# The first weight chunk third in the load stream and split in halves, the first four products filled two input blocks at a time

## What is computed

```python
mod_lat = silu_c @ w_ada[l] + b_ada[l]          # modulation of the 256 tokens
mod_ctx = silu_cc @ w_ada[l] + b_ada[l]         # modulation of the context
sh, sc, gt = jnp.split(mod_lat, 3, axis=-1)
sh_c, sc_c, gt_c = jnp.split(mod_ctx, 3, axis=-1)
xn = _rms_norm(x, g_norm) * (1 + sc[:, None]) + sh[:, None]
cn = _rms_norm(ctx, g_norm) * (1 + sc_c) + sh_c
(au, av, az, bq, bk, bv, bz, cq, ck, cv, co, cz, cg) = _split_proj(xn @ w_in)
(au_c, ..., ck_c, ...)                               = _split_proj(cn @ w_in)
```

## Time and profile before

| | us |
|---|---|
| median of three runs | 1150.38 |
| lowest, highest | 1149.53, 1152.26 |
| the profiled execution | 1150.57 |
| its span in the trace | 1148.6 |
| busy in it: TensorE matmuls | 1093.4 |
| VectorE, ScalarE, GpSimd | 722.2, 590.7, 130.0 |

### The profile page before, as it was taken

One profiled execution on the slowest core, in us unless ns is written; L12 is line 12 of the kernel. 1 busy time (PEld: TensorE's weight loads), 2 busy tenths in 40 slices (PEclk: granted clock), 3 DMA queues, 4 the chain that ended last, 5 costly groups with the idle time before them and its releaser, 6 DMA issues.

```text
span 1148.6 us, 19921 instructions
## 1 busy us (share of the span) xinstructions
PE 1093.4 (95%) x8128; PEld 958.1 (83%) x8128; DVE 722.2 (63%) x1227; ACT 590.7 (51%) x969; POOL 130.0 (11%) x156
## 2 busy tenths in 40 slices
PE   3999999999989999889999999999998999999998
PEld 1787888766767989579888999999997789999997
DVE  4546557376434667766866667666676667766764
ACT  5343666445233567656556555444465536544443
POOL 0000000044020000233223100000012321000000
PEclk9999999999898999989999999999999999999999
DMA  9732112177420433014433345555543233555451
GB/s 371 268 137 79 68 43 74 41 278 270 147 74 1 160 144 116 33 55 157 179 125 114 144 147 221 184 185 182 184 149 119 101 115 143 200 187 200 182 187 54
DMA packets 24426, 167.01 MB, mean 145 GB/s; under 512 B 2832, under 2 KB 3216, under 8 KB 4752
## 3 DMA queue, kind: packets, MB, share of 16 engines
q1 hardware_dynamic: 24336, 165.74, 39.4%
HBM read 164.68 MB, written 1.05 MB: 144 GB/s over the span
## 4 chain that ended last, share of the span: by engine, by line
PE 86%; DVE 5%; ACT 4%; issue 2%; POOL 1%; DMA 1%; SPq 0%; DVEq 0%; ACTq 0%; POOLq 0%
PE bank L426 24%; PE bank L427 23%; PE bank L428 23%; DVE wlo L420 2%; ACT whi L405 2%; PE bank L464 2%; PE bank L1373 2%; PE bank L1506 1%; PE bank L1526 1%; PE bank L1516 1%; PE bank L1400 1%; PE bank L1391 1%; DMA raw<-in_stream 1%; PE bank L479 1%; PE bank L2455 1%
## 5 line engine op out<-in xcount | busy, mean ns | idle before, releaser
L426 PE MATMUL bank<-OPH,whi 128*128 128x256 f32 (+1 forms) x1716 | 526.5, 307 | 5.8 <-DVE wlo L420 3.4
L427 PE MATMUL bank<-OPL,whi 128*128 128x256 f32 (+1 forms) x1716 | 516.7, 301 | 0.0
L428 PE MATMUL bank<-OPH,wlo 128*128 128x256 f32 (+1 forms) x1716 | 516.5, 301 | 0.0
L420 DVE TENSOR_TENSOR wlo<-raw,whi 128x1024 fp32r<-128x1024 f32 x256 | 305.3, 1234 | 109.5 <-ACT whi L405 109.3
L426 PEld LDWEIGHTS bank<-OPH,whi 128*128 128x128 f32 x1716 | 329.3, 192 | 27.8 <-issue 7.6
L427 PEld LDWEIGHTS bank<-OPL,whi 128*128 128x128 f32 x1716 | 329.4, 192 | 12.5 <-issue 1.7
L428 PEld LDWEIGHTS bank<-OPH,wlo 128*128 128x128 f32 x1716 | 329.2, 192 | 11.5
L405 ACT ACTIVATE whi<-raw 128x1024 fp32r<-128x1024 f32 x256 | 255.6, 1049 | 103.8 <-PE bank L428 103.8
L426 PE MATMUL bank<-whi,OPH 128*128 128x256 f32 (+1 forms) x272 | 89.2, 328 | 0.0
L427 PE MATMUL bank<-wlo,OPH 128*128 128x256 f32 (+1 forms) x272 | 87.3, 321 | 0.0
L428 PE MATMUL bank<-whi,OPL 128*128 128x256 f32 (+1 forms) x272 | 87.1, 320 | 0.0
(11 more groups left out here) (284 smaller groups left out, 1167.1 us busy)
## 6 DMA issues: line engine op xcount, KB each, us to landing
raw<-in_stream SPq DMA_DIRECT2D x147, 1024.0 KB, 4.8
PROJ<-in_stream SPq DMA_DIRECT2D x5, 1024.0 KB, 14.9
X<-in_x_in SPq DMA_DIRECT2D x4, 512.0 KB, 6.3
C<-in_con SPq DMA_DIRECT2D x1, 1477.5 KB, 9.1
out<-PROJ SPq DMA_DIRECT2D x4, 256.0 KB, 2.0
WST<-in_w_s SPq DMA_DIRECT2D x2, 256.0 KB, 5.0
PROJ<-in_last_gain SPq DMA_DIRECT2D x1, 512.0 KB, 5.7
BS<-in_b_s SPq DMA_DIRECT2D x1, 256.0 KB, 5.3
```

Of the source, the lines that this page charges most:

```text
L420: nc.vector.tensor_tensor(c.w[1][:, part], c.raw[:, part], c.w[0][:, part].bitcast(F32), ALU.subtract).then_inc(*raises(c.lo[h]))
L426: nc.tensor.matmul(out, w[0], x[0], start=start, stop=False, skip_group_check=skip)
L427: nc.tensor.matmul(out, w[0], x[1], start=False, stop=False, skip_group_check=skip)
L428: return nc.tensor.matmul(out, w[1], x[0], start=False, stop=stop, skip_group_check=skip)
```

## The change

Three things are moved; no instruction is added or taken away.

The stream: weight chunk 0 comes before the two chunks of pair 1 and no longer behind them. Weight chunk 1 stays the sixth.

The split: ScalarE and VectorE split the first half of weight chunk 0 before the operand of pair 0, its second half behind that, the first half of weight chunk 1 before the operand of pair 1 (low part: before `dve_operand(e, 1)`), its second half behind that as before.

TensorE's order: ck0 on blocks (0, 1) goes between the products and the turn of pair 1; ck1, keys and values on (0, 1) follow the turn; then the four products take the next two blocks in turn between the steps of pairs 2 and 3.

```diff
                 pairs[1].multiply(e, 0)
                 pairs[1].multiply(e, 1)
+                first.fill_part(e, ck0, (0, 1))
                 pairs[1].turn(e)
-                for j in (ck0, ck1):
-                    first.fill_part(e, j, (0, 1))
+                first.fill_part(e, ck1, (0, 1))
+                first.fill_part(e, keys, (0, 1))
+                first.fill_part(e, values, (0, 1))
                 pairs[2].multiply(e, 0)
-                for j in (ck0, ck1):
-                    first.fill_part(e, j, (2, 3))
+                first.fill_part(e, ck0, (2, 3))
+                first.fill_part(e, ck1, (2, 3))
                 pairs[2].multiply(e, 1)
-                first.fill_part(e, keys, (0, 1))
+                first.fill_part(e, keys, (2, 3))
                 pairs[2].turn(e)
-                first.fill_part(e, keys, (2, 3))
+                first.fill_part(e, values, (2, 3))
                 pairs[3].multiply(e, 0)
-                first.fill_part(e, values, (0, 1))
+                first.fill_part(e, ck0, (4, 5))
+                first.fill_part(e, ck1, (4, 5))
                 pairs[3].multiply(e, 1)
-                first.fill_part(e, values, (2, 3))
+                first.fill_part(e, keys, (4, 5))
                 pairs[3].turn(e)
-                for j in (ck0, ck1, keys, values):
-                    first.fill_part(e, j, (4, 5))
+                first.fill_part(e, values, (4, 5))
                 for j in (ck0, ck1, keys, values):
                     first.fill_part(e, j, (6, 7))
...
                 pairs[0].copy_rows(e, "act")
+                split_hi(e, 0.5)
                 act_operand(e, 0)
+                split_hi(e, 1)
                 pairs[1].copy_rows(e, "act")
-                split_hi(e, 1)
+                split_hi(e, 1.5)
                 act_operand(e, 1)
                 split_hi(e, 2)
...
                 dve_scale(e, 0)
+                split_lo(e, 0.5)
                 dve_operand(e, 0)
+                split_lo(e, 1)
                 pairs[1].add_bias(e)
                 dve_scale(e, 1)
-                split_lo(e, 1)
+                split_lo(e, 1.5)
                 dve_operand(e, 1)
                 split_lo(e, 2)
...
-        pairs = []
+        pairs, early = [], []
...
-            if i == 1:
-                early = take(2)
+            if i < 2:
+                early += take(1)
...
-            s += [ada[pairs[:4]], w_in[:2], ada[pairs[4:8]], w_in[2:], ada[pairs[8:]],
+            s += [ada[pairs[:2]], w_in[:1], ada[pairs[2:4]], w_in[1:2], ada[pairs[4:8]], w_in[2:], ada[pairs[8:]],
```

## The result

The changed kernel takes 1152.49 us in the median of 20 runs (1148.39 to 1154.22), the kernel before 1149.72 us beside it (1148.50 to 1152.26, 20 runs). The ratio is 1.0019 with a 95% interval of 1.0011 to 1.0026: **2.2 us slower**, within the 0.2% bound but clear of no change. The forecast was 1150.7, 0.3 us over the 1150.38 of its time, so the loss is 1.9 us larger than forecast. The time lies in the stated range, next to the 1152.6 that rival B gave for one spell of low clock.

A forecast was written before the change was run, and what follows sets the result against it. TensorE, busy 95% of the span, was taken as the bound. Keys at 31.25 + 25.72 of work + waits 0.92 + 2.12 = 60.01 against 59.69, +0.3 us: 1150.7 us, range 1148.2 to 1153.8.

The forecast's parts named there:

- rival B: Clock falls in TensorE's new waits (29.3 to 31.25 or 52.4 to 54.5 us): one spell +2.2, 1152.6 us; chance 0.27.
- The mark: Start of the gate product on TensorE, at 59.69 us before the change; forecast 60.01, with nothing behind it edited.
- Part 1: Weight chunk 0 as third load instead of fifth lands at 18.3 us instead of 23.4; pair 1's second chunk at 23.4.
- Part 2: Split in halves on ScalarE and VectorE: first high half fits ScalarE's gap; low operand starts at 24.4 instead of 23.62 us.
- Part 3: TensorE's ck0 ahead of pair 1's turn: turn at 26.9 instead of 24.85, keys wait until 31.25, 1.9 us idle.
- the assumption on the clock: Between 23 and 26.2 us TensorE is busy longer, so the clock holds; a fall there would cost 0.6 us.
- Part 4: TensorE's fills of blocks 4 and 6 come before their low operands: waits of 0.92 and 2.12 us.
- The sum: Start of keys, unchanged work and two operand waits put the gate product at 60.01 against 59.69 us: +0.3 us.
- A: Rival that the forecast's addition up to the gate product holds: 1150.7 us; chance 0.50.
- C: Rival that the operand waits before blocks 4 and 6 do not come: 1147.7 us in full; chance 0.13.
- D: Rival that chunk 0's landing does not follow its new place, holding back ScalarE's first operand: +1.8, 1152.5 at least; chance 0.04.

The follow-up runs named there:

- the last experiment: Eight float32 matmuls that nobody reads put ahead of the first product: on the changed kernel 1152.51 us, ratio 1.0014; on the kernel with early pairs 1147.07 us.

## Why the prediction was right, and where it was not

**The mark and the mechanism.** Right: the difference arises ahead of the gate product, and the 1089 us behind it moved by 0.1. The time came 1.9 us over the forecast, and the range held because it had been drawn wide enough for rival B.

**Part 1, the stream.** Right. In the changed kernel's trace the weight chunk is issued at 5.44 us and takes 12.7 us, landing at 18.1 (18.3 forecast); pair 1's second product starts at 23.19 (23.5 forecast).

**Part 2, the split.** Right. The first high half runs at 19.62 in ScalarE's gap, the low operand starts at 24.11 (24.4).

**Part 3, TensorE's order.** Right in its mechanism, 1.64 us off in size. The turn behind the fill at 27.82, MOD at 29.55 (27.95 forecast), the scaling at 30.03, the low half at 31.62 and keys at 32.89 make the chain that was forecast, link by link; with the clock held it starts keys at 31.03. The sentence that failed is the assumption on the clock: "I take it that the clock holds there", with "0.6 us" if not. The price counted only block k1 and the turn. The fall came earlier, at 22.1 us, in the stretch between pair 1's two products that part 1 itself had opened; so pair 1's second product (0.87 us more) and both blocks of ck0 fell in it as well: the turn started 0.92 us later than forecast, and MOD followed it by 1.73 us instead of 1.05. The reading behind the assumption failed too. The prediction says that the trace of before shows a fall only after long idleness, but there the clock fell at 26.2, 0.3 us after the turn had ended at 25.9; the long wait of 3.37 us had only begun, and what lay behind the fall was an idle stretch of 1.84 us, no longer than the 1.9 and 2.1 us that the new order was forecast to have.

**Part 4, the operands too late.** Right. Both waits came where they were placed, 0.97 and 1.96 us for 0.92 and 2.12, and went in the experiment that moves the turns. From the turn to the fill it was 4.41 us both times, where 4.30 were forecast.

**The sum.** From keys to the mark 28.76 us were forecast and 29.40 measured, though the two waits are 0.11 shorter than forecast. The missing 0.75 us are small terms. The two waits cost more than the profile's idle time: from start to start they add 1.04 and 2.13 us (46.70 less 44.66 and the 1.00 of a product in a running stream; 56.65 less 54.29 and 0.23), 0.24 us over the idle times. Behind both, the two blocks start 0.79 and 0.80 us apart (46.70 and 47.49, 56.65 and 57.45), where three matmuls at 0.228 take 0.68; that makes 0.23 us, which the prediction named, at 0.1 us at most, and left out. The restart at keys and one more change from fills to a product cost about 0.1 us each. The rest, under 0.1 us, is not placed. With 1.64 us from the clock in part 3 that makes 2.28 us, and 60.01 + 2.28 is the measured 62.29.

**The rivals.** B was the one that came, at half of A's chance: a spell of low clock, in a third place. That its +2.2 us is what was measured is partly luck: in the profile the clock cost 1.64 us and not 1.86, and the small terms above, which B did not have, made up the difference and more. It was given 0.27; over the 20 runs only two, at 1148.39 and 1148.65 us, have a mean clock of 0.990, and 15 lie above 1151.9; the median is 1152.5 at a mean clock of 0.987 (eight runs) and 1153.3 at 0.982 (two). Two runs thus lie 2 us under the forecast of A, and no trace tells where their clock held. B's chance should have been the larger. C did not happen; D did not either, and its mechanism is real when the stream is put back.

**The rule on the clock.** The Trainium skill, "TensorE: Matmul & The Clock Gate", section "A second HAM failure mode: psum-queue depth-cycling", has brief idle stretches between groups of matmuls, when they come often enough, make the clock swing between its levels. The traces agree in part. The clock fell in or behind idle stretches of 1.36, 1.87 and 1.96 us, and at none of those places in the profile with all stretches filled. But the changed kernel's own wait of 1.96 us and waits of 1.87 and 1.97 us in the last experiment brought no fall, so the length of the stretch alone does not decide, and what does is open. The prediction took from this rule a time of one or two spells, and the time was that of one.

## What to carry to other kernels

Moving work ahead of a wait did not pay here, because what it displaced was itself a producer: the turns of pairs 2 and 3 feed an operand 4.4 us later, and a fill put in front of them turned cover into a wait. Try the steps with the longest chain behind them first, as early as their loads allow, and the fills behind; with the same loads and the same split that gave 1147.1 us instead of 1152.5. And when one long idle stretch becomes several short ones, price a fall of the clock as a likely case, with all the work that would run under it: in this stage it fell at least once in eleven of the twelve profiles.

## What was not expected of the hardware

The clock's fall comes at different times under the same instructions: in the kernel before at 26.2 us, in its version with fewer filling matmuls at 20.3, though these begin only at 23.2. Runs of one kernel spread over 8.4 us (1146.89 to 1155.31, one stretch filled) and 8.7 us (1147.26 to 1155.95, the changed kernel with the eight matmuls in front), with the mean clock between 0.994 and 0.981. A profile is one draw of this: the medians of the two kernels are 2.8 us apart, and their runs spread over 5.8 us (changed) and 3.8 us (before).

A float32 matmul of 512 columns shows as two matmuls and took 0.81 to 0.95 us at the high level (2.84 us for three; 5.70 us from the first of seven to the next instruction), about four times the 0.23 us of one with split operands.
